# Two transformer blocks in one program: reordered waits, output projections begun with finished pairs, one sum for two norms, modulation summed earlier

## The chip, the core and the metric

The program runs on one core of one Trainium2 chip, as one launch. The metric is the device time in microseconds (us); lower is better. TensorE (PE) multiplies, VectorE (DVE), ScalarE (ACT) and GpSimd (POOL) do elementwise work, SyncE (SP) issues most of the loads. Each engine executes its own instructions in order and waits on semaphores.

## What is computed

A sequence of 256 tokens with 1024 features goes through two blocks of two layers each, all in float32:

```python
# first block
x = x + delta_net(rms_norm(x, a_norm))           # stage A: in-projection, causal conv of 4 taps + silu,
                                                 #   gated delta rule with 8 heads, rms_norm * silu(z), out-projection
k, v = rms_norm(x, kv_norm) @ w_kv               # stage B: one x, two gains
q, z = rms_norm(x, b_norm) @ w_in
x = x + (attention(q, k, v, bias) * silu(z)) @ w_out
x = rms_norm(x, final_norm)
# second block: mod = silu(c) @ ada_w[i] + ada_b[i]; shift, scale, gate = split(mod, 3)
h = rms_norm(x, norm[0]) * (1 + scale) + shift   # stage C
x = x + gate * (retention(rope(q, k), v) * silu(g)) @ w_out
h = rms_norm(x, norm[1]) * (1 + scale) + shift   # stage D: attention with 16 heads, normed q and k
x = x + gate * (attention(...) * silu(g)) @ w_out
```

## The kernel before

**Jobs and chunks.** All arrays lie with features on the 128 partitions. The projections are cut into 104 jobs of 256 output features, numbered through: 0 to 15 in-projection of A, 16 to 19 its out-projection (`JOB_OUT_A`), 20 to 35 in-projections of B (`JOB_B`), 36 to 39 `JOB_OUT_B`, 40 to 63 C, 64 to 67 `JOB_OUT_C`, 68 to 99 D, 100 to 103 `JOB_OUT_D`. A job reads one weight chunk of 1 MB (two in the out-projections of C and D), 112 chunks in all. SP loads chunk c into the buffer `raw` (three slots, so it first waits until chunk c-3 has been split); ACT writes the rounded high part `whi` (`high(c)`, two instructions), DVE the rest `wlo` (`low(c)`, two instructions); both parts have room for two chunks. PE multiplies high by high, high by low and low by high, so a job is 48 matmuls of 256 columns (96 with two chunks), on the two banks ps0 and ps1 in turn. `job(J, ..., ready=, split=)` waits before a tile of its input for `h_ok_sem` or `o_split_sem`. The activations are split in high and low in the same way (`hhi`, `hlo` for the normed input, `ohi`, `olo` for the mixer's output).

**The order is written out by hand.** Each engine has one block of code, and what stands ahead in it runs first. There is no scheduler.

**Stage A.** For job J of 0 to 7 ACT does `high(J + 1)`, the first tap of the convolution of job J (L943), the silu of job J-1 (L948) and for odd J the square of a pair of keys (L953); DVE adds the other three taps (L1283). After each odd job PE sums the squares (`key_sums`). Then comes the delta rule: six levels of a blockwise inversion, each with half of one job before and half behind it (`parts`), over banks that are taken in turn (`slot`, ps6 and ps7). The finished pairs of heads are normed and split by DVE (`split_o`), and `JOB_OUT_A` follows, whose first job waits for each pair.

**Norms.** PE sums the squares of x over the partitions with a matrix of ones (`sums`, `x_sums`), ACT forms the reciprocal root with Ln and Exp (`rsqrt`), DVE scales x tile by tile and takes the rests (`prepare`, L1251 and L1245 or L1247), ACT rounds (`split_h`). In B `prepare` runs twice, with gain `b_norm` and then `kv_norm`, and each run has a `low` of a weight chunk in its middle or behind it. Between B and C two norms follow each other; the kernel forms the squares of x and of x times `final_norm` and two sums, and passes a value from ACT to DVE and back (L1155 to L1162, L1514, L1517). The normed x itself (`final_x`, L1523) is written by DVE during C.

**Attention of B and D, retention of C.** Pair i's softmax, transposes (`turn`, L724) and mixing (`mix`) run during the jobs of pair i+1. After the last pair nothing is left to overlap: PE does `turn` and `mix` and waits for DVE's `finish` (or `finish_c` in C) before the out-projection.

**Modulation.** ada_w is loaded in 48 units of 512 KB into `ring` (two slots). For a unit POOL does one multiply and three adds (`ada_unit`, L373 to L381), PE then one matmul with ones (`ada(u)`), and after six units DVE adds the bias (`take_mod`). SP issues unit u beside a chunk: u of 0 to 17 beside chunks 21 to 38, 18 to 41 beside 40 to 63, the last six in D; unit u waits until POOL has finished unit u-2. POOL starts them after it has spread the two bias tables to DRAM (`scr_d` 4 MB, `scr_b` 2 MB, L391 and L393), read one back and prepared the rope angles (L401 to L426).

## Time and profile before

| what | value |
|---|---|
| median of the runs | 971.07 us |
| the runs | 965.6, 971.07, 971.14 us |
| the profiled execution, its own time | 969.52 us |
| its span on the core | 967.6 us |
| mean granted clock of TensorE | 0.956 of full speed |

The profile comes from one execution. Its span is 1.9 us shorter than that execution's own time; all times inside the trace are counted from the start of the span. Matmul ends are modelled, so only the starts, and the idle time in square brackets before an instruction, are used for TensorE.

### The profile page before, as it was taken

How to read it: one execution, taken by the hardware profiler on the slowest of the kernel's cores; microseconds unless marked ns; L12 is line 12 of the kernel's file. 1: busy time of each engine (PE TensorE's matmuls, PEld its weight loads, DVE VectorE, ACT ScalarE, POOL GpSimd, SP SyncE). 2: the span in 40 equal slices, each digit the busy share in tenths (PEclk: the TensorE clock that was granted, in tenths of full speed). 3: DMA queues.
4: the chain of work that ended last, by engine and by line, in shares of the span. 5: the costliest groups of instructions: out<-in, count | busy, mean ns of one | idle time of the engine just before them, and what ended most of it. 6: DMA issues, size and time to landing. Idle time of an engine off the chain costs nothing.

```text
span 967.6 us, 16171 instructions
## 1 busy us (share of the span) xinstructions
PE 878.0 (91%) x6762; PEld 847.1 (88%) x6762; DVE 586.5 (61%) x803; ACT 478.0 (49%) x736; POOL 299.6 (31%) x238
## 2 busy tenths in 40 slices
PE   4989999999829999789996989699899999999798
PEld 4788899997729999679996989699899999999698
DVE  3675545336696677459977677644567555655643
ACT  4554454444426555345333343423676666766531
POOL 1100000000496878363984767020144300000000
PEclk8997999999979999798997999999999999999999
DMA  6332299542645666154764645285255534425250
GB/s 247 128 130 96 54 142 173 124 116 89 232 153 192 218 244 240 66 196 136 272 226 163 212 171 215 87 282 195 111 189 204 194 136 172 154 109 174 89 189 29
DMA packets 28247, 158.42 MB, mean 164 GB/s; under 512 B 3456, under 2 KB 3984, under 8 KB 13840
## 3 DMA queue, kind: packets, MB, share of 16 engines
q1 hardware_dynamic: 24816, 146.37, 42.3%
q0 software_dynamic: 3360, 11.03, 7.1%
q8 instruction: 53, 0.87, 0.4%
q14 instruction: 18, 0.15, 0.0%
HBM read 150.04 MB, written 7.34 MB: 163 GB/s over the span
## 4 chain that ended last, share of the span: by engine, by line
PE 85%; DVE 9%; ACT 3%; issue 2%; DMA 1%; DVEq 0%; SPq 0%; ACTq 0%
PE ps L448 83%; DVE wlo L1219 2%; DVE arena L1251 2%; PE ps L632 1%; PE ps L724 1%; DVE olo L1264 1%; DVE arena L1538 1%; DVE hlo L1245 1%; ACT whi L874 1%; DMA x<-x_t 1%; DVE ohi L1262 0%; DVE arena L1534 0%; DVE olo L1245 0%; ACT L863 0%; ACT early L953 0%
## 5 line engine op out<-in xcount | busy, mean ns | idle before, releaser
L1219 DVE TENSOR_TENSOR wlo<-raw,whi 128x1024 fp32r<-128x1024 f32 x224 | 310.4, 1423 | 179.2 <-ACT whi L874 179.0
L448 PE MATMUL ps<-hhi,whi 128*128 128x256 f32 x960 | 286.4, 298 | 43.1 <-ACT arena L1097 17.6
L874 ACT ACTIVATE whi<-raw 128x1024 fp32r<-128x1024 f32 x224 | 225.9, 1051 | 106.5 <-PE ps L448 73.6
L448 PE MATMUL ps<-hlo,whi 128*128 128x256 f32 x960 | 278.3, 290 | 0.0
L448 PE MATMUL ps<-hhi,wlo 128*128 128x256 f32 x960 | 277.9, 290 | 0.0
L448 PEld LDWEIGHTS ps<-hhi,whi 128*128 128x128 f32 x960 | 191.4, 199 | 47.0 <-issue 29.0
L448 PEld LDWEIGHTS ps<-hlo,whi 128*128 128x128 f32 x960 | 191.6, 200 | 2.0 <-issue 1.9
L448 PEld LDWEIGHTS ps<-hhi,wlo 128*128 128x128 f32 x960 | 191.0, 199 | 0.0
L448 PE MATMUL ps<-ohi,whi 128*128 128x256 f32 x512 | 149.0, 291 | 16.0 <-DVE olo L1264 11.6
L373 POOL TENSOR_TENSOR ada_ring<-ada_ring,sil 128x1024 f32<-128x1024 f32 x48 | 101.8, 2121 | 170.6 <-DMA ada_ring<-ada 170.6
L448 PE MATMUL ps<-olo,whi 128*128 128x256 f32 x512 | 146.3, 286 | 0.0
L448 PE MATMUL ps<-ohi,wlo 128*128 128x256 f32 x512 | 146.2, 286 | 0.0
L448 PEld LDWEIGHTS ps<-ohi,whi 128*128 128x128 f32 x512 | 99.8, 195 | 18.9 <-DVE olo L1264 11.9
L448 PE MATMUL ps<-arena 128*128 128x128 f32 (+2 forms) x656 | 103.9, 308 | 1.8 <-ACT arena L1079 1.2
L448 PEld LDWEIGHTS ps<-arena 128*128 128x128 f32 x656 | 94.5, 200 | 9.7 <-issue 3.4
L448 PEld LDWEIGHTS ps<-olo,whi 128*128 128x128 f32 x512 | 99.9, 195 | 0.2 <-issue 0.2
L448 PEld LDWEIGHTS ps<-ohi,wlo 128*128 128x128 f32 x512 | 99.7, 195 | 0.0
L448 PE MATMUL ps<-whi,hhi 128*128 128x256 f32 x320 | 94.6, 296 | 0.0
L448 PE MATMUL ps<-wlo,hhi 128*128 128x256 f32 x320 | 90.5, 283 | 0.0
L448 PE MATMUL ps<-whi,hlo 128*128 128x256 f32 x320 | 90.5, 283 | 0.0
L375 POOL TENSOR_TENSOR ada_ring<-ada_ring 128x512 f32<-128x512 f32 x48 | 76.6, 1596 | 3.8
L448 PEld LDWEIGHTS ps<-whi,hlo 128*128 128x128 f32 x320 | 61.4, 192 | 1.9 <-issue 1.9
(190 smaller groups left out, 1045.9 us busy)
## 6 DMA issues: line engine op xcount, KB each, us to landing
raw<-weights SPq DMA_DIRECT2D x112, 1024.0 KB, 5.1
ada_ring<-ada SPq DMA_DIRECT2D x48, 512.0 KB, 5.9
bias_rows_d<-ada_ring POOLq DMA_DIRECT2D x1, 4096.0 KB, 45.9
bias_rows_b<-fb POOLq DMA_DIRECT2D x1, 2048.0 KB, 86.7
arena<-bias_rows_d POOLq DMA_DIRECT2D x2, 1024.0 KB, 10.1
x<-x_t SPq DMA_DIRECT2D x2, 512.0 KB, 4.5
arena<-bias_rows_b POOLq DMA_DIRECT2D x1, 1024.0 KB, 7.1
arena<-bias_rows_d POOLq DMA_DIRECT2D x2, 512.0 KB, 13.3
```

Source lines behind the costliest of these rows:

```text
L373: pool.tensor_tensor(b, b, sil[:, :].unsqueeze(2).to_broadcast([P, KT, P]), ALU.mult).then_inc(ada_step_sem, 1)
L375: pool.tensor_tensor(b[:, 0:4, :], b[:, 0:4, :], b[:, 4:8, :], ALU.add).then_inc(ada_step_sem, 1)
L448: return pe.matmul(o, l, r, start=start, stop=stop, skip_group_check=skip)
L632: m = pe.transpose(b[:, m4 * P:m4 * P + P], tt[:, 4 * g + m4, :], ident)
L724: m = pe.transpose(turned_bank(hh, soft0)[:, a * P:a * P + P], ts[:, hh, c0:c0 + P], ident)
L874: act.activation(whi[:, unit % UNITS, :, :], raw[:, c % RAW, 4 * half:4 * half + 4, :], ACT.Copy).then_inc(hi_ok_sem, 1)
L1219: dve.tensor_tensor(wlo[:, unit % UNITS, :, :], raw[:, c % RAW, 4 * half:4 * half + 4, :], whi[:, unit % UNITS, :, :].bitcast(F32), ALU.su ...
L1245: dve.tensor_tensor(lo[:, t, :], f[:, t, :], hi[:, t, :].bitcast(F32), ALU.subtract).then_inc(h_ok_sem, 1)
L1251: dve.scalar_tensor_tensor(out=f[:, t, :], in0=x[:, t, :], scalar=gain(t), in1=rs, op0=ALU.mult, op1=ALU.mult).then_inc(hf_ok_sem, 1)
L1264: return dve.tensor_tensor(olo[:, r, :], src, ohi[:, r, :].bitcast(F32), ALU.subtract)
L1538: own(dve.scalar_tensor_tensor(out=of[:, t, :], in0=of[:, t, :], scalar=col("ret_gn", 4 * h + k), in1=zs_c[:, 4 * (h % 2) + k, :], op0=ALU ...
```

## The change

1. **Start.** The eight tiles of squares of x are added in pairs by DVE first, so that PE sums four. The first `low` moves behind the first scaled tile.
2. **Key squares.** In jobs 0 to 7 ACT does silu(J-1) and the key square ahead of the first tap of job J.
3. **Modulation.** Units 0 to 29 are loaded from chunk 11 on, three beside a chunk, and summed by POOL before and behind the spreading of the bias tables; PE takes six units at each of the levels 2, 4 and 6 of the delta rule, six after job 17 and six after job 19. `ada_sum` has 12 slots instead of 6. The bias rows lie in memory that `ohi` uses later, so DVE waits for the spread (`scr_out_sem`) before the first `split_o`; reading one table back and the rope angles come behind unit 29. Units 30 to 41 follow in B and its out-projection, none in C; the last six stay in D.
4. **Shared middle input.** x times the root is formed once for B (four instructions of two tiles), and the gains of q and of k/v are applied while ACT rounds and DVE takes the rests; the `low`s in between move ahead or behind.
5. **Out-projections.** The last `turn` and `mix` of B and D are issued inside the first job of the out-projection, before tiles 4 and 6 of B and 8 and 12 of D; that job waits pair by pair. In C the last sum is issued before tile 8.
6. **One sum for two norms.** The product of the two roots is formed from one sum, with the square root of the squared gain plus eps (`gq`) as scale of the square; the plain sum, needed for `final_x` alone, is formed in C from two added tiles; `final_x` moves from h = 0, 1 to h = 1, 2.
7. Several `high` and `low` of the next chunk move ahead of a norm or a finish.

```diff
+        turn_order = ["keys0", "keys1"]
+        for lv in range(1, LEVELS):
+            turn_order += [f"level{lv}_{g}" for g in range(4)]
+            turn_order += {1: ["values0"], 2: ["mod0"], 3: ["values1"], 4: ["values2", "mod1"], 5: ["values3"], 6: ["mod2"]}[lv]
+        turn_order += [f"sum{i}" for i in range(4)]
...
-                    if c == (JOB_B + 1 + u if u < 18 else JOB_C + (u - 18) if u < 42 else 76 + 2 * (u - 42)):
-                        if u < 2:
-                            sp.wait_ge(o_split_sem, 4)
-                            sp.wait_ge(scr_out_sem, 32)
-                        else:
+                    if c == ((11, 11, 12, 12, 12)[u] if u < 5 else 13 + (u - 5) // 3 if u < 26 else u - 6 if u < 42 else 76 + 2 * (u - 42)):
+                        if u >= 2:
                             sp.wait_ge(ada_mul_sem, u - 1)
                         sp.dma_start(ring[:, u % 2, :, :].rearrange("p a b -> p (a b)"), ada_w[u]).then_inc(ada_in[u % 2], 16)
...
-                if u >= 6:
-                    pool.wait_ge(ada_used_sem, u - 5)
-                pool.tensor_tensor(ada_sum[:, u % 6, :], b[:, 0, :], b[:, 1, :], ALU.add).then_inc(ada_mul_sem, 1)
+                if u >= 12:
+                    pool.wait_ge(ada_used_sem, u - 11)
+                pool.tensor_tensor(ada_sum[:, u % 12, :], b[:, 0, :], b[:, 1, :], ALU.add).then_inc(ada_mul_sem, 1)
...
+            pool.wait_ge(sil_ok_sem, 1)
+            pool.wait_ge(conv_ok_sem, 8)
+            for u in range(6):
+                ada_unit(u)
             pool.wait_ge(fd_ok_sem, 2)
             pool.wait_ge(nt_ok_sem, 4)
             pool.dma_start(scr_d.rearrange("p h t -> h p t"), fd[:, :].unsqueeze(1).to_broadcast([16, P, 512])).then_inc(scr_out_sem, 16)
             pool.wait_ge(bias_sb_sem, 1)
             pool.dma_start(scr_b.rearrange("p h t -> h p t"), fb[0:8, :].unsqueeze(1).to_broadcast([8, P, 512])).then_inc(scr_out_sem, 16)
+            for u in range(6, 30):
+                ada_unit(u)
             pool.wait_ge(scr_out_sem, 32)
...
-            for u in range(42):
+            pool.wait_ge(h_ok_sem, 24)
+            for u in range(30, 42):
...
+                            if kx in at:
+                                at[kx]()
+                            if split is not None and kx % heads == 0:
+                                pe.wait_ge(o_split_sem, split + kx // heads + 1)
...
-            def ada(u):
-
-                if u % 6 == 0:
-                    pe.wait_ge(mod_ok_sem, u // 6)
+            def ada(u, bank=ps[7]):
+
+                if u % 6 == 0 and u >= 24:
+                    pe.wait_ge(mod_ok_sem, u // 6 - 3)
                 pe.wait_ge(ada_mul_sem, u + 1)
-                mm(ps[7][:, u % 6:u % 6 + 1], ada_sum[:, u % 6, :], ones[:, 0:1], True, True).then_inc(ada_used_sem, 1)
+                mm(bank[:, u % 6:u % 6 + 1], ada_sum[:, u % 12, :], ones[:, 0:1], True, True).then_inc(ada_used_sem, 1)
...
-            sums(lambda t: xsq_a[:, t, :], 8, S, sq_ok_sem, lambda t: t // 2 + 1)
+            sums(lambda t: xsq_a[:, 4 * (t // 2) + t % 2, :], 4, S, sq_ok_sem, lambda t: t // 2 + 1)
...
+                if lv in (2, 4, 6):
+
+                    b = taken(slot_of_mod(lv // 2 - 1))
+                    for u in range(3 * lv - 6, 3 * lv):
+                        ada(u, b)
...
+                for u in {JOB_OUT_A + 1: range(18, 24), JOB_OUT_A + 3: range(24, 30)}.get(J, ()):
+                    ada(u)
...
+            turn_last, mix_last = attend(JOB_B, 4, 0, 4, (ohi[:, 8:16, :], olo[:, 8:16, :]), (hhi, hlo), False, (8, 16), ada_b)
             for J in range(JOB_OUT_B, JOB_C):
-                job(J, "T", ohi, olo)
-                if J < JOB_OUT_B + 3:
-                    ada(2 * J - 60)
-                    ada(2 * J - 59)
-
-            pe.wait_ge(ss_read_sem, own_ss[0])
-            for t in range(KT):
-                pe.wait_ge(sq_ok_sem, 8 + t + 1 - t % 2)
-                mm(ssb[:, 0:S], ones[:, :], xsq[:, t, :], t == 0, False)
-                pe.wait_ge(sq_ok_sem, 8 + t + 2 - t % 2)
-                m = mm(ssb[:, S:2 * S], ones[:, :], xsq2[:, t, :], False, t == KT - 1)
-            m.then_inc(ss_ok_sem, 1)
-            own_ss[0] += 1
-
+                if J == JOB_OUT_B:
+                    job(J, "T", ohi, olo, split=4, at={4: turn_last, 6: mix_last})
+                else:
+                    job(J, "T", ohi, olo)
+                if J == JOB_OUT_B + 1:
+                    for u in range(39, 42):
+                        ada(u)
+
+            x_sums(2)
...
+                    sums(lambda t: xsq[:, 6 + t, :], 2, S, m1_add_sem, lambda t: 2)
...
+                if J == JOB_OUT_C:
+                    job(J, "T", ohi, olo, split=8, at={8: lambda: sums_c(3)}, heads=4)
...
+                if J == JOB_OUT_D:
+                    job(J, "T", ohi, olo, split=12, at={8: turn_last, 12: mix_last})
...
             for J in range(8):
                 high(J + 1)
-                first_tap(J)
                 if J:
                     silu(J - 1)
                 if J % 2:
                     key_square(J // 2)
+                first_tap(J)
                 if J == 1:
...
+                split_c(J0 + 4 * pairs, 1)
...
+            for dst, gain in ((ohi[:, 8:16, :], "b_norm"), (hhi, "kv_norm")):
+                for t in range(KT):
+                    act.wait_ge(hf_ok_sem, 8 + t // 2 + 1)
+                    act.activation(dst[:, t, :], hf[:, t, :], ACT.Copy, scale=col(gain, t)).then_inc(hh_ok_sem, 1)
...
+            square_x(JOB_OUT_B, gain=lambda t: gq[:, t:t + 1])
...
-            act.activation(rsb[:, 0, :], ssb[:, 0:S], ACT.Ln, scale=1.0 / D, bias=epsc[:, 0:1]).then_inc(fin_ln_sem, 1)
-            act.wait_ge(fin_ln_sem, 1)
-            act.activation(rsb[:, 1, :], rsb[:, 0, :], ACT.Exp, scale=-1.0).then_inc(ss_read_sem, 1)
-            act.activation(rsb[:, 2, :], rsb[:, 0, :], ACT.Exp, scale=-0.5).then_inc(r1_ok_sem, 1)
-            act.wait_ge(fin_mid_sem, 1)
-            act.activation(rsb[:, 3, :], rsb[:, 3, :], ACT.Ln, scale=1.0 / D, bias=epsc[:, 0:1]).then_inc(fin_ln_sem, 1)
-            act.wait_ge(fin_ln_sem, 2)
-            act.activation(rsb[:, 3, :], rsb[:, 3, :], ACT.Exp, scale=-0.5).then_inc(rs_ok_sem, 1)
+            act.activation(rsb[:, 1, :], ssb[:, 0:S], ACT.Ln, scale=1.0 / D, bias=epsc[:, 3:4]).then_inc(ss_read_sem, 1)
+            act.wait_ge(ss_read_sem, ss_n[0])
+            act.activation(rsb[:, 1, :], rsb[:, 1, :], ACT.Exp, scale=-0.5).then_inc(rs_ok_sem, 1)
             split_h(3, hf, hhi, shift=lambda t: mod[:, t:t + 1])
+            for n in range(4):
+                act.activation(xsq[:, 2 * n:2 * n + 2, :], x[:, 2 * n:2 * n + 2, :], ACT.Square).then_inc(m1_sq_sem, 1)
...
+            for t in range(2):
+                dve.wait_ge(xsq_ok_sem, 2 * t + 2)
+                dve.tensor_tensor(xsq_a[:, 4 * t:4 * t + 2, :], xsq_a[:, 4 * t:4 * t + 2, :], xsq_a[:, 4 * t + 2:4 * t + 4, :], ALU.add).then_inc(sq_ok_sem, 1)
             next_rs()
-            low(0)
-            prepare(0, lambda t: col("a_norm", t), None, hf_a, rs_a, hhi, hlo)
+            prepare(0, lambda t: col("a_norm", t), None, hf_a, rs_a, hhi, hlo, between=lambda: low(0), after=0)
...
+            def mod_of_slot(i):
+
+                b, free, n = slot(slot_of_mod(i))
+                dve.wait_ge(ada_used_sem, 6 * i + 6)
+                a0 = COLS["ada_b"] + 6 * i
+                dve.tensor_tensor(mod[:, 6 * i:6 * i + 6], b[:, 0:6], cols[:, a0:a0 + 6], ALU.add).then_inc(free, 1)
...
+                if lv in (2, 4):
+                    mod_of_slot(lv // 2 - 1)
...
+            dve.wait_ge(scr_out_sem, 32)
...
+                    if J in (JOB_OUT_A + 2, JOB_OUT_B + 2):
+                        take_mod(3 if J < JOB_B else 6)
+                    for c in chunks_of(J):
+                        if n or c > chunks_of(J0)[0] or J0 == JOB_OUT_A:
+                            low(c + 1)
...
+                low(chunks_of(J0 + 4 * pairs)[0] + 1)
...
-            prepare(1, lambda t: col("b_norm", t), None, hf, rsb[:, 0, :], ohi[:, 8:16, :], olo[:, 8:16, :])
-            low(JOB_B + 1)
-            prepare(2, lambda t: col("kv_norm", t), None, hf, rsb[:, 0, :], hhi, hlo, between=lambda: low(JOB_B + 2))
+
+            def lo_of(prep, t, gain, hi, lo):
+
+                dve.wait_ge(hh_ok_sem, 8 * prep + t + 1)
+                dve.scalar_tensor_tensor(out=lo[:, t, :], in0=hf[:, t, :], scalar=col(gain, t), in1=hi[:, t, :].bitcast(F32), op0=ALU.mult, op1=ALU.subtract).then_inc(h_ok_sem, 1)
+
+            for n in range(4):
+                dve.tensor_tensor(hf[:, 2 * n:2 * n + 2, :], x[:, 2 * n:2 * n + 2, :], wide(rsb[:, 0, :], 2), ALU.mult).then_inc(hf_ok_sem, 1)
+                if n:
+                    for t in (2 * n - 2, 2 * n - 1):
+                        lo_of(1, t, "b_norm", ohi[:, 8:16, :], olo[:, 8:16, :])
+            for t in (6, 7):
+                lo_of(1, t, "b_norm", ohi[:, 8:16, :], olo[:, 8:16, :])
+            for t in range(KT):
+                lo_of(2, t, "kv_norm", hhi, hlo)
+            low(JOB_B + 2)
...
-            dve.wait_ge(ss_read_sem, rs_n[0] + 1)
-            dve.tensor_tensor(rsb[:, 3, :], ssb[:, S:2 * S], rsb[:, 1, :], ALU.mult).then_inc(fin_mid_sem, 1)
-            dve.wait_ge(r1_ok_sem, 1)
+            low(JOB_C + 1)
...
+                if h in (1, 2):
+                    if h == 1:
+                        dve.wait_ge(r1_ok_sem, 1)
+                    final_x(4 * h - 4)
+                    final_x(4 * h - 3)
```

On the DMA queue of SyncE, from the first weight chunks to chunk 22, before:

```order
L326 DMA raw<-weights 128x2048 x21
L340 DMA ada_ring<-ada 128x1024
L326 DMA raw<-weights 128x2048
L340 DMA ada_ring<-ada 128x1024
L343 DMA arena<-positions 128x256
```

and now:

```order
L340 DMA raw<-weights 128x2048 x11
L351 DMA ada_ring<-ada 128x1024 x2
L340 DMA raw<-weights 128x2048
L351 DMA ada_ring<-ada 128x1024 x3
L340 DMA raw<-weights 128x2048
L351 DMA ada_ring<-ada 128x1024 x3
```

The modulation loads begin with chunk 11 instead of chunk 21, and three of them stand between one weight chunk and the next.

On TensorE, the end of level 2 of the delta rule (four transposes of `tt` and the first matmuls of the job behind), before:

```order
L448 MATMUL ps<-arena 128x64 x4
L632 MATMUL ps<-cst,arena 128x128 x4
L448 MATMUL ps<-hhi,whi 128x256
L448 MATMUL ps<-hlo,whi 128x256
L448 MATMUL ps<-hhi,wlo 128x256
```

and now, with the six matmuls of `ada` between them:

```order
L466 MATMUL ps<-arena 128x64 x4
L652 MATMUL ps<-cst,arena 128x128 x4
L466 MATMUL ps<-ones,ada_sum 128x1 x6
L466 MATMUL ps<-hhi,whi 128x256
L466 MATMUL ps<-hlo,whi 128x256
```

The same six stand at levels 4 and 6; all that PE does behind them waits until POOL has finished the sixth unit.

On ScalarE, one pair of jobs in stage A (L943/L958 first tap, L948/L963 silu, L953/L968 key square, L874/L886 `high`), before:

```order
L874 ACTIVATE whi<-raw 128x1024 x2
L943 ACTIVATE arena<-ps,columns 128x256 x2
L948 ACTIVATE arena<-arena 128x512
L953 ACTIVATE early<-arena 128x512
L874 ACTIVATE whi<-raw 128x1024 x2
```

and now:

```order
L886 ACTIVATE whi<-raw 128x1024 x2
L963 ACTIVATE arena<-arena 128x512
L968 ACTIVATE early<-arena 128x512
L958 ACTIVATE arena<-ps,columns 128x256 x2
L886 ACTIVATE whi<-raw 128x1024 x2
```

The square no longer stands behind the tap that waits for the end of the odd job.

## Rows read from the trace of the kernel before

**Rows 1.** The page, part 1: busy time, share of the span, instructions.

```profile
PE 878.0 (91%) x6762; PEld 847.1 (88%) x6762; DVE 586.5 (61%) x803; ACT 478.0 (49%) x736; POOL 299.6 (31%) x238
```

**Rows 2.** Waits of TensorE: line, releaser, us in total, times, longest.

```profile
PE ps L448 <- ACT early L953: 8.4, 4, 2.1
...
PE ps L724 <- DVE arena L1453: 7.1, 2, 3.6
```

**Rows 3.** Timeline of TensorE after the first key sums, then in full flow: start, us.

```profile
40.13 0.41 PE L448 MATMUL ps<-hhi,wlo 128*128 128x256 f32 x1
40.34 0.41 PE L448 MATMUL ps<-hhi,whi 128*128 128x256 f32 x1
...
50.04 0.28 PE L448 MATMUL ps<-hlo,whi 128*128 128x256 f32 x1
50.16 0.28 PE L448 MATMUL ps<-hhi,wlo 128*128 128x256 f32 x1
```

**Rows 4.** Timeline: last tap of a key convolution, its square, the key sums.

```profile
49.71 0.47 DVE L1283 SCALAR_TENSOR_TENSOR arena<-ps,columns,arena 128x253 f32<-128x253 f32 x1
...
54.02 0.63 ACT L953 ACTIVATE early<-arena 128x512 f32<-128x512 f32 x1
...
54.70 1.05 PE L448 MATMUL ps<-ones,early 128*128 128x1 f32 x8 [2.11 <-ACT early L953]
```

**Rows 5.** The chain that ended last, levels 4 and 6 of the delta rule: start, us.

```profile
170.51 10.13 PE ps L448 x88
...
199.82 26.48 PE ps L448 x206
```

**Rows 6.** Tile raw on the DMA queue of SyncE, 100 to 230 us.

```profile
L326 SPq DMA_DIRECT2D raw<-weights x7: 327/328/328, 118.1 to 207.4; - x7
...
DMA to landing us min/median/max: 5.0/16.9/23.1
```

**Rows 7.** Timeline of SyncE: the load of weight chunk 23.

```profile
251.18 0.33 SPq L326 DMA_DIRECT2D raw<-weights  x1
```

**Rows 8.** The page, part 6: DMA issues, count, KB each, median us to landing.

```profile
ada_ring<-ada SPq DMA_DIRECT2D x48, 512.0 KB, 5.9
bias_rows_d<-ada_ring POOLq DMA_DIRECT2D x1, 4096.0 KB, 45.9
bias_rows_b<-fb POOLq DMA_DIRECT2D x1, 2048.0 KB, 86.7
```

**Rows 9.** Timeline of GpSimd: spread tables, then starts of modulation units.

```profile
116.42 1.11 POOL L391 DMA_DIRECT2D bias_rows_d<-ada_ring  x1 [80.31 <-DVE arena L1349]
...
273.24 2.08 POOL L373 TENSOR_TENSOR ada_ring<-ada_ring,sil 128x1024 f32<-128x1024 f32 x1
...
278.15 1.89 POOL L373 TENSOR_TENSOR ada_ring<-ada_ring,sil 128x1024 f32<-128x1024 f32 x1
...
470.75 2.03 POOL L373 TENSOR_TENSOR ada_ring<-ada_ring,sil 128x1024 f32<-128x1024 f32 x1
...
496.04 2.87 POOL L373 TENSOR_TENSOR ada_ring<-ada_ring,sil 128x1024 f32<-128x1024 f32 x1
```

**Rows 10.** Timeline of VectorE: one step of the second preparation of x.

```profile
284.70 2.11 DVE L1251 SCALAR_TENSOR_TENSOR arena<-x,columns,arena 128x256 f32<-128x256 f32 x1
```

**Rows 11.** Timeline of TensorE: first matmul behind five gaps.

```profile
291.06 0.58 PE L448 MATMUL ps<-hhi,whi 128*128 128x256 f32 x1 [17.65 <-ACT arena L1097]
...
436.81 0.55 PE L448 MATMUL ps<-hhi,whi 128*128 128x256 f32 x1 [6.20 <-DVE hlo L1247]
...
524.74 0.55 PE L448 MATMUL ps<-hhi,whi 128*128 128x256 f32 x1 [7.62 <-DVE wlo L1219]
...
628.20 0.58 PE L448 MATMUL ps<-ohi,whi 128*128 128x256 f32 x1 [6.11 <-DVE olo L1264]
...
917.87 0.39 PE L448 MATMUL ps<-ohi,whi 128*128 128x256 f32 x1 [1.97 <-DVE olo L1264]
```

**Rows 12.** Timeline of TensorE: sum of squares before the middle projections.

```profile
252.01 3.62 PE L448 MATMUL ps<-arena,ones 128*128 128x256 f32 x16
```

More of the change, by code:

```diff
@@ L150, in two_blocks @@
         rt16 = A(9216, 4, S, parts=16)
-        ada_sum = sb("ada_sum", [P, 6, P])
+        ada_sum = sb("ada_sum", [P, 12, P])
         lmask = sb("lmask", [P, LEVELS, 256], U8)
@@ L228, in two_blocks @@
         sq_ok_sem = sem("sq_ok")
+        xsq_ok_sem = sem("xsq_ok")
+        gq_ok_sem = sem("gq_ok")
+        m1_sq_sem = sem("m1_sq")
+        m1_add_sem = sem("m1_add")
         ss_ok_sem = sem("ss_ok")
@@ L455, in bank_empty, with job @@
                     pe.wait_ge(bank_free[J % 2], max(J // 2 - 6, 0))
-            def job(J, form, hi, lo, ready=None, split=None):
+            def job(J, form, hi, lo, ready=None, split=None, at={}, heads=2):
                 bank = v2(pj[J % 2])
@@ L904, in split_h, with square_x @@
                         act.activation(dst[:, t, :], src[:, t, :], ACT.Identity, bias=shift(t)).then_inc(hh_ok_sem, 1)
-            def square_x(J0, second=False):
+            def square_x(J0, gain=None):
                 for n in range(4):
@@ L1195, in _ @@
             attend(JOB_D, 8, 4, 12, True)
-            for J in range(JOB_OUT_D, N_JOBS):
-                for c in chunks_of(J):
-                    high(c + 1)
+            for c in range(chunks_of(JOB_OUT_D)[1], N_CHUNKS):
+                high(c + 1)
         @block.vector
@@ L1238, in wide, with prepare @@
                 return v.unsqueeze(1).to_broadcast([P, n, v.shape[-1]])
-            def prepare(prep, gain, shift, f, rs, hi, lo, between=None):
+            def prepare(prep, gain, shift, f, rs, hi, lo, between=None, after=3):
                 def lo_part(t):
@@ L1253, in prepare @@
                         lo_part(t - 1)
-                    if t == 3 and between is not None:
+                    if t == after and between is not None:
                         between()
@@ L1473, in attend @@
                         lows(J + 1)
-                    if not normed and i == 2:
-                        take_mod(0)
                     lows(J + 2)
@@ L1504, in gains_of_c @@
             def gains_of_c():
-                take_mod(2)
-                dve.wait_ge(mod_ok_sem, 3)
+                for i in range(3):
+                    dve.wait_ge(slot(slot_of_mod(i))[1], slot(slot_of_mod(i))[2] + 1)
                 scaled_gain(0)
```

157 lines of the change are left out of this document (81 added, 76 removed).

## The prediction

> **What bounds the kernel now.** I read the page's busy shares first: TensorE is busy for 878 of 967.6 us, no other engine for two thirds [rows 1]. So the time is what TensorE must do plus what it waits, and the second view is its waits by releaser: four of 2.1 us for key squares and two of up to 3.6 us for the last softmax of B and D [rows 2]; the timeline gives the single long ones, 17.65 us in B (put down to L1097, though the second preparation of x ends just before), 6.2, 7.6, 6.1 and 2.0 us [rows 11]. A gap costs more than its length: behind the first key sums the matmuls of 256 columns start 0.21 us apart, in full flow 0.12 us [rows 3], the two levels of the clock, 1.2 and 2.4 GHz. Such a stretch takes some 12 matmuls, so each gap costs 1 to 2 us behind it. In the delta rule the chain runs through TensorE throughout, a level in 14.7 us [rows 5] (two levels from 170.5 to 199.8). There TensorE has no gap, and everything put in its way there is paid in full.
>
> **Part 1 and 2, start and key squares.** TensorE's 8 sums of float32 squares took 6.0 us at the slow clock; four take 3.0, the two additions of DVE add some 0.7 in front, and the moved low part brings the first matmul forward by about 0.5: gain 2.5 us (estimate). For the key squares the question is whether they can be ready at the end of the odd job. The last tap of the even job's convolution begins at 49.7 and ends at 50.2, and silu and square take about 1.2 us more, so 51.4; the odd job ended at 52.6, 2.1 us before the key sums at 54.7, and the square began only at 54.0 [rows 4]. So all four waits of 2.1 us go, each with its slow stretch (12 matmuls at 0.09 us, and key sums at half speed, together 1.5 us): 4 x 3.6 = 14.5 us. What is late next is the low part for the next job; per pair DVE needs 9.5 us of about 12. Bounds: 8.4 us (the waits alone) and 18. Together with the start the delta rule begins 17 us earlier.
>
> **Part 3, modulation.** Nothing is saved by itself: 48 units before and after, 30 of them now before B. A unit costs GpSimd 4.9 us with a quiet VectorE and 6.3 us beside a busy one (25.3 us for four) [rows 9]; 5.0 to 5.5 in the delta rule. Thirty take 150 to 165 us. The first loads are issued with chunk 11, which I place at 72 us, the first unit is done at 83, the sixth at about 113 (the load of the sixth stands behind chunk 13, which waits for `low(10)`). Only then GpSimd spreads the bias tables, at about 114, nearly the absolute time of before, 116.4 [rows 9], while TensorE is 17 us further on. Level 2 (124 us) finds its six units ready. Level 4 is reached at 170.5 - 17 = 153.5 us [rows 5] and needs unit 11.
>
> The spread is the trouble. While it ran (landed 45.9 and 86.7 us after issue [rows 8], so until 204 us) weight chunks took 5.0 to 23.1 us from issue to landing, median 16.9 [rows 6]; modulation loads in their own, calmer stretch took 5.9 [rows 8]. The ring has two slots, and a load goes out when the unit two before is done, so at a landing time of 16.9 two units pass per 16.9 + 4.9 = 21.8 us. By that alone: unit 7 is done at 124, units 8 and 9 at 143 and 148, 10 and 11 at 165 and 170: level 4 waits 17 us. Level 6 comes 29.3 us later, at 200; unit 17 is done at about 219: 19.7 us. Counting also that a load stands behind its chunk on the one queue (chunk 14 issued at 121 lands at 143, then unit 8 at 149, unit 9 at 155), unit 11 is done at about 181 and unit 17 at 231: 28 and 20 us. After the spread GpSimd keeps pace (unit 23 before the end of job 17). Unit 29, however, is loaded beside chunk 23, and that waits for `low(20)`, which ended at 251.2 us [rows 7], as the last job of the out-projection ended at 252.0 [rows 12]. Load 6, unit 5: TensorE waits 10 to 11 us there in any case, ahead of the sum of squares. Stalls in all: 17 + 19.7 + 10.8 = 47.5 or 28 + 20 + 11 = 59; I take 53, as the truth about the queue lies between, and 4 us for the slow clock behind three stalls. The lower bound is the 11 us alone. That DVE waits for the spread before its first `split_o` costs nothing: the spread ends at 205 to 210, the split comes after the stalls.
>
> The Trainium skill (SBUF — State Buffer, "Who interferes with whom") says that a VectorE instruction with two inputs in SBUF and a GpSimd instruction that reads SBUF lock each other out for their whole length. The trace agrees: a scaling of one tile, 0.47 us elsewhere, took 2.11 us beside a unit [rows 10].
>
> **Part 4, shared middle input.** From the end of the sum of squares at 255.6 [rows 12] to the third job of B at 291.1 [rows 11] passed 35.4 us for two jobs of TensorE. DVE was the bound: 32 tile steps stretched by GpSimd's units (2.11 us for one [rows 10]), and two low chunks between. Now DVE has 4 double steps of 0.69 and 16 of 0.47 us, and units wait for `h_ok` 24, so only the rope angles run beside it, as they did beside the first preparation before. TensorE is then the bound: 2 us to the first matmul, 11.5 for two jobs, 1 to 2 for the slow clock and 1 for the root, 15.8 us. Gain 19.6, less 2 us because the sum of squares now follows a stall at the slow clock, plus 1.7 for the slow start of job 22 in the old order: 19 us. Bounds: 10 (DVE still stretched) and 21.
>
> **Part 5, out-projections.** B: the gaps were 3.6 [rows 2], 0.6 and 2.0 us. Four tiles (2.9 us) cover the first, two more (1.4) the second; the wait for the last pair stays, since two tiles are less than mix and finish. Gain 3.5 and some 1.5 of clock: 5 us. D: eight tiles (5.8 us) and four (2.9) cover all; 5.6 + 1.4 = 7 us [rows 11] (the last gap ended at 917.9). C: gaps of 0.6, 1.3 and 6.1 us, the last before 628.2 [rows 11]; twelve tiles now run ahead of the last pair, and DVE's finish of 5.7 us still leaves some 4 us: gain 5.5 with the units gone from there.
>
> **Part 6, one sum.** Eight fewer sums in the open: 3.5 us. The gap of 6.2 before 436.8 [rows 11] shrinks to the 2.7 of a single root: 3.5. Clock 1, two sums and squares added in C 0.9: gain 7. Bounds 3 and 9. **C itself** has no units left: the 7.6 us before 524.7 [rows 11] came from DVE steps stretched by them as in rows 10: two `final_x` and two low chunks stand there between the finish and the next job, 5.6 us more than undisturbed (estimate). Gain 5.6 and 2.6 of clock; the shorter gap in h = 2 stays, as `final_x` comes there: 8 us.
>
> **Sum**, against the profiled execution (969.5 us of its own, 967.6 span; the median of the runs is 971.1): -17 + 53 + 4 - 19 - 5 - 7 - 8 - 5.5 - 7 = -11.5. From the median: **960 us**.
>
> **Rivals.** (a) *The loads are quick*: the slow landings were those of single 1 MB chunks, and half-size loads slip through in 6 us. Then level 4 and 6 wait for nothing and only the 11 us remain: -17 + 11 + 1 - 19 - 32.5 = -56, 915 us. For it speaks that chunks in that stretch moved in a few us once they began; against it the median of 16.9 us over seven, one of which was issued at 207.4, after the spread [rows 6, 8]. (b) *Half of it*, the stalls at levels 4 and 6 together about 20 us: 937 us. (c) *Each load waits its own turn behind the spread.* If what is queued does not follow at once but pays about 13.5 us again each (21.7 us for a chunk, less the 7 it moves), then between 114 and 205 only some six loads come through, three of them chunks: unit 11 is done at about 211, level 4 waits 57 us, the rest 14: -17 + 71 + 5 - 19 - 32.5 = +8, 979 us. It decides against the change from 62 us of stalls on. Units at 6.3 us throughout would add 10 more: 989. (d) *The gains do not come*: the key waits stay (the squares still late): +14 on the forecast, 974.
>
> The Trainium skill (DMA: Bandwidth & Descriptors, "Queues, rings and completion order") says that each DMA engine takes turns between queues a whole packet at a time, typically 9 to 17 descriptors. That is rival (c) as a mechanism. No row here shows two loads of one queue waiting together, so the trace leaves it open.
>
> **Chances.** Forecast (948 to 970) 0.42; (a) 0.17; (b) 0.17; (c) 0.15 with its worse end; (d) and others 0.09. The range leaves out the fastest third of (a) and the worst end of (c): 912 to 982. A measurement of this kernel tells a change of about 1% from none. Faster by over 1% (below 961.4): (a), (b) and just over half of the forecast, 0.57; within 1%: 0.31; slower: 0.12.
>
> **What the new profile would show.** No wait behind L968's square; a wait of TensorE for GpSimd's `ada_sum` of 15 to 30 us at level 4 (about 154 us), 15 to 20 at level 6 and about 11 after job 19; modulation loads of 12 to 20 us in the spread; in B about 16 us from the root to the third job; no wait over 3 us in h = 1 of C; a gap of 2.7 us before C; no gap over 1 us in D's out-projection. I am wrong if the loads land in 6 us during the spread (then 915), or if unit 11 is done after 190 us.

## The result

The changed kernel takes 977.99 us (median of 5 runs, 974.07 to 979.3), the kernel before 970.35 us (5 runs). The ratio is 1.0079 with a 95% interval of 1.0047 to 1.0112: **slower by 0.8%**, where 960 us, faster by 1%, was forecast. The profiled execution took 977.0 us, its span is 975.2.

The page of the changed kernel, parts 1 and 4 (busy time, the chain that ended last). Against [rows 1] TensorE and VectorE work less, and yet the span is longer. The loads of the modulation now stand in the chain with 8%, GpSimd's four steps with 3, 2, 1 and 1%.

```profile
PE 873.1 (90%) x6742; PEld 843.5 (87%) x6742; DVE 552.6 (57%) x793; ACT 481.0 (49%) x740; POOL 279.1 (29%) x239
...
PE ps L466 71%; DMA ada_ring<-ada 8%; POOL ada_ring L385 3%; DVE wlo L1248 2%; POOL ada_ring L387 2%; POOL ada_ring L389 1%; DVE olo L1293 1%; ACT whi L886 1%; PE ps L751 1%; DVE ohi L1291 1%; DVE arena L1456 1%; DVE arena L1594 1%; ACT L875 1%; DVE hlo L1276 1%; POOL ada_sum L393 1%
```

TensorE's waits in the changed kernel: line, releaser, us in total, times, longest. The key squares of [rows 2] are gone, and of the two waits for the last softmax the one in B has shrunk to 0.7 us and the one in D is gone. One row replaces them, 47.2 us for the modulation sums, and VectorE's last output parts (`olo`) cost 13.4.

```profile
PE ps L466 <- POOL ada_sum L393: 47.2, 6, 20.9
PE ps L466 <- DVE olo L1293: 13.4, 7, 3.9
PE ps L466 <- DVE arena L1298: 8.2, 1, 8.2
PE ps L466 <- DVE hlo L1276: 7.9, 3, 4.6
PE ps L466 <- DVE wlo L1248: 5.3, 3, 2.4
```

**Where the time stands, stage by stage.** The timeline of TensorE has the same landmark instructions in both kernels. The table sets their starts side by side; the difference between two rows of the last column is what the stage between them gained or lost.

| landmark | before | after | after - before |
|---|---|---|---|
| first projection matmul | 18.94 | 16.97 | -2.0 |
| first matmul of the delta rule (L605, now L625) | 115.85 | 102.19 | -13.7 |
| projection in level 4 | 170.27 | 201.75 | +31.5 |
| projection in level 6 | 199.58 | 236.49 | +36.9 |
| first job of A's out-projection | 226.58 | 265.74 | +39.2 |
| sum of squares ahead of B | 252.01 | 312.70 | +60.7 |
| first job of B | 258.18 | 322.32 | +64.1 |
| scores of B's first pair | 304.42 | 346.78 | +42.4 |
| sum of squares ahead of C | 423.54 | 457.61 | +34.1 |
| first job of C [rows 11] | 436.81 | 465.81 | +29.0 |
| behind the shorter middle gap of C | 571.84 | 590.82 | +19.0 |
| first job of D | 682.81 | 697.42 | +14.6 |
| last matmul's end | 964.2 | 971.8 | +7.6 |

Up to the delta rule 13.7 us are gained, from there to B 77.8 are lost, and from B on 56.5 are gained again. Such differences between two single traces are uncertain by 2 to 3 us: two kernels of the experiments below, with the same code up to there, began the delta rule at 98.00 and 100.29 us.

The stalls in level 4, timeline of TensorE of the changed kernel (start, us, in brackets the idle time and its releaser). Three waits, 35.9 us, and then matmuls 0.21 us apart: the granted clock of this stretch (163 to 202 us) is 0.52 of full speed, the lower of the two levels.

```profile
167.61 0.58 PE L466 MATMUL ps<-ones,ada_sum 128*128 128x1 f32 x2 [3.38 <-POOL ada_sum L393]
189.06 0.59 PE L466 MATMUL ps<-ones,ada_sum 128*128 128x1 f32 x2 [20.87 <-POOL ada_sum L393]
201.30 0.58 PE L466 MATMUL ps<-ones,ada_sum 128*128 128x1 f32 x2 [11.65 <-POOL ada_sum L393]
201.75 0.56 PE L466 MATMUL ps<-hhi,whi 128*128 128x256 f32 x1
202.11 0.41 PE L466 MATMUL ps<-hlo,whi 128*128 128x256 f32 x1
202.32 0.41 PE L466 MATMUL ps<-hhi,wlo 128*128 128x256 f32 x1
```

What GpSimd waited for there, from the chain that ended last (start, us, what): a load, the four steps of a unit (4.6 to 6.7 us together), the next load.

```profile
128.70 27.55 DMA ada_ring<-ada
...
156.31 4.04 POOL ada_ring L385
...
163.06 21.32 DMA ada_ring<-ada
...
189.03 16.33 DMA ada_ring<-ada
```

Loads of 512 KB that landed in a median of 5.9 us in [rows 8] took 21.3 to 29.2 us from issue to landing while the spread ran (four, issued from 128 to 168 us; a fifth, issued at 189, took 16.3 and landed as the spread ended at 205), and 3.3 to 5.7 us from then on (issues from 201 us on). Unit 11 was done at 201.

### The profile page after: what moved, and what is told of

The parts are those of the page before. It is cut to its first block, busy times and chain, and to the rows that moved or that the text cites. A ratio compares the mean times of both kernels' runs of the same rounds, so it can differ in the third digit from the quotient of the medians.

```text
span 975.2 us, 16128 instructions
## 1 busy us (share of the span) xinstructions
PE 873.1 (90%) x6742; PEld 843.5 (87%) x6742; DVE 552.6 (57%) x793; ACT 481.0 (49%) x740; POOL 279.1 (29%) x239
## 4 chain that ended last, share of the span: by engine, by line
PE 71%; DVE 8%; DMA 8%; POOL 6%; ACT 3%; issue 2%; SPq 0%; DVEq 0%; ACTq 0%; POOLq 0%
PE ps L466 71%; DMA ada_ring<-ada 8%; POOL ada_ring L385 3%; DVE wlo L1248 2%; POOL ada_ring L387 2%; POOL ada_ring L389 1%; DVE olo L1293 1%; ACT whi L886 1%; PE ps L751 1%; DVE ohi L1291 1%; DVE arena L1456 1%; DVE arena L1594 1%; ACT L875 1%; DVE hlo L1276 1%; POOL ada_sum L393 1%
## 5 line engine op out<-in xcount | busy, mean ns | idle before, releaser
L1248 DVE TENSOR_TENSOR wlo<-raw,whi 128x1024 fp32r<-128x1024 f32 x224 | 294.1, 1352 | 181.1 <-ACT whi L886 181.0
L886 ACT ACTIVATE whi<-raw 128x1024 fp32r<-128x1024 f32 x224 | 225.7, 1052 | 78.6 <-PE ps L466 60.8
L466 PEld LDWEIGHTS ps<-hhi,whi 128*128 128x128 f32 x960 | 189.7, 198 | 22.8 <-issue 21.8
L466 PE MATMUL ps<-ohi,whi 128*128 128x256 f32 x512 | 150.6, 294 | 16.4 <-DVE olo L1293 13.4
L466 PE MATMUL ps<-olo,whi 128*128 128x256 f32 x512 | 148.3, 290 | 0.0
L466 PE MATMUL ps<-ohi,wlo 128*128 128x256 f32 x512 | 148.2, 289 | 0.0
L466 PEld LDWEIGHTS ps<-ohi,whi 128*128 128x128 f32 x512 | 101.8, 199 | 18.9 <-issue 11.2
L466 PEld LDWEIGHTS ps<-olo,whi 128*128 128x128 f32 x512 | 101.9, 199 | 0.0
L466 PEld LDWEIGHTS ps<-ohi,wlo 128*128 128x128 f32 x512 | 101.7, 199 | 0.0
L466 PE MATMUL ps<-arena 128*128 128x128 f32 (+2 forms) x656 | 99.4, 300 | 0.7 <-ACT arena L1219 0.7
L466 PEld LDWEIGHTS ps<-arena 128*128 128x128 f32 x656 | 91.7, 194 | 7.4 <-issue 3.5
L387 POOL TENSOR_TENSOR ada_ring<-ada_ring 128x512 f32<-128x512 f32 x48 | 71.3, 1485 | 3.8
```

Source lines behind the costliest of these rows:

```text
L387: pool.tensor_tensor(b[:, 0:4, :], b[:, 0:4, :], b[:, 4:8, :], ALU.add).then_inc(ada_step_sem, 1)
L466: return pe.matmul(o, l, r, start=start, stop=stop, skip_group_check=skip)
L886: act.activation(whi[:, unit % UNITS, :, :], raw[:, c % RAW, 4 * half:4 * half + 4, :], ACT.Copy).then_inc(hi_ok_sem, 1)
L1248: dve.tensor_tensor(wlo[:, unit % UNITS, :, :], raw[:, c % RAW, 4 * half:4 * half + 4, :], whi[:, unit % UNITS, :, :].bitcast(F32), ALU.su ...
```

## The experiments

**Give the modulation back.** The changed kernel, with the modulation in B and C as before and everything else kept:

```diff
-if c == ((11, 11, 12, 12, 12)[u] if u < 5 else 13 + (u - 5) // 3 if u < 26 else u - 6 if u < 42 else 76 + 2 * (u - 42)):
+if c == (JOB_B + 1 + u if u < 18 else JOB_C + (u - 18) if u < 42 else 76 + 2 * (u - 42)):
...
-                    for u in range(3 * lv - 6, 3 * lv):
-                        ada(u, b)
...
             pool.wait_ge(h_ok_sem, 24)
-            for u in range(30, 42):
+            pool.wait_ge(sil_ok_sem, 1)
+            for u in range(42):
```

> The changed kernel with the modulation as in the kernel before: loads, units, sums and additions all in B and C again, everything else of the change kept. Theory (the moved modulation alone turned the gain into a loss: 45 us of waits and slow clock at levels 4 and 6, 4 in level 1, 10 in the out-projection of A, 14 after it): 978 - 69 = 909, plus about 12 for units that disturb VectorE in C again, 921 us. Rival (the time of the units only changes place, and 42 units beside B and C cost there what they cost in the delta rule): 955 to 975 us.

Measured 931.71 us (928.07 to 934.08), ratio to the kernel before 0.9592 (0.9553 to 0.9631). The moved modulation alone costs 978.0 - 931.7 = 46 us, and the rest of the change gains 38.5. The first theory holds, 11 us off. B's first job begins 79.5 us earlier than in the changed kernel (242.77 us), but the units then cost 15 us between there and C and 16 us behind it, where I had allowed 12. Two waits of VectorE's low part in the middle of C are back, 5.6 and 7.7 us; TensorE's waits:

```profile
PE ps L461 <- DVE wlo L1250: 15.3, 5, 7.7
PE ps L461 <- DVE hlo L1278: 11.9, 5, 7.4
```

From B's first job on, this kernel gains 26 us over the kernel before, where the changed kernel gains 56.5. Stage by stage, by the landmarks of the table: 19.8 us up to the scores of B's first pair, 0.7 from there to C, 1.6 lost in C, 7.0 gained in D. In the changed kernel the same four are 21.8, 13.4, 14.4 and 7.0.

**The key squares alone**, on the kernel before:

```diff
                 high(J + 1)
-                first_tap(J)
                 if J:
                     silu(J - 1)
                 if J % 2:
                     key_square(J // 2)
+                first_tap(J)
```

> The kernel before with only the order of ScalarE changed: silu and key square ahead of the next job's first tap. Theory (the four waits of 2.1 us go, each with its slow stretch): 970.4 - 14 = 956 us, no wait of TensorE for the square. Rival (the low parts or the convolution become late instead, and half of it stays): 963 us or more.

Measured 956.03 us (952.24 to 957.68), ratio 0.984 (0.9802 to 0.9878): 14.1 us under the 970.15 of the kernel before beside it, and no wait for the square is left among TensorE's waits. Four waits of 2.1 us were worth 14, since each had its slow stretch behind it: matmuls 0.21 us apart in the kernel before [rows 3], while here the granted clock from 48 to 60 us, around the second key sums, is 1.00.

**The spread ahead of the units.** The two table spreads go out while the key jobs run:

```diff
+            pool.wait_ge(fd_ok_sem, 2)
+            pool.dma_start(scr_d.rearrange("p h t -> h p t"), fd[:, :].unsqueeze(1).to_broadcast([16, P, 512])).then_inc(scr_out_sem, 16)
+            pool.wait_ge(bias_sb_sem, 1)
+            pool.dma_start(scr_b.rearrange("p h t -> h p t"), fb[0:8, :].unsqueeze(1).to_broadcast([8, P, 512])).then_inc(scr_out_sem, 16)
             pool.wait_ge(sil_ok_sem, 1)
             pool.wait_ge(conv_ok_sem, 8)
             for u in range(6):
                 ada_unit(u)
-            pool.wait_ge(fd_ok_sem, 2)
-            pool.wait_ge(nt_ok_sem, 4)
-            pool.dma_start(scr_d.rearrange("p h t -> h p t"), fd[:, :].unsqueeze(1).to_broadcast([16, P, 512])).then_inc(scr_out_sem, 16)
-            pool.wait_ge(bias_sb_sem, 1)
-            pool.dma_start(scr_b.rearrange("p h t -> h p t"), fb[0:8, :].unsqueeze(1).to_broadcast([8, P, 512])).then_inc(scr_out_sem, 16)
```

> The changed kernel with the spread of both bias tables issued during the key and query jobs, ahead of the first unit, instead of behind the sixth. Theory (the spread delays the loads of units 8 to 11): they land in about 6 us, no wait at level 4 or 6, and GpSimd is far enough ahead that it disturbs A's out-projection less: 978 - 38 - 3 - 4 = 933 us, more if the key jobs now wait for their chunks. Rival (the two ring slots and the one queue with the chunks hold the loads back, the spread matters little): still 20 us or more of waits for the sums, 960 to 978 us.

Measured 947.19 us (945.76 to 949.4), ratio 0.9749 (0.9713 to 0.9786). No wait for a unit is left at levels 4 and 6, and the modulation loads from 85 to 200 us landed in a median of 3.8 us, so the spread is what held them back. The result is 14 us above the 933 expected; they went into the stretch that the spread now fills (34.9 to 125.7 us). The delta rule began 8 us later, and level 2 waited 6.5 us for units 4 and 5. The view of tile `raw`, 15 to 100 us, shows weight chunks that took a median of 15.7 us there (4.9 in the changed kernel):

```profile
DMA to landing us min/median/max: 4.8/15.7/25.1
```

ScalarE waited twice for a chunk, 10.6 us in all, with a key square behind its high part, and TensorE for that square. TensorE's waits:

```profile
PE ps L465 <- POOL ada_sum L393: 17.0, 5, 5.9
PE ps L465 <- DVE olo L1292: 12.7, 5, 3.9
PE ps L465 <- DVE hlo L1275: 7.9, 3, 4.6
PE ps L465 <- ACT early L967: 6.0, 1, 6.0
```

**Does GpSimd itself cost anything?** Units 0 to 5 and 18 to 29 do 2 of their 128 columns in the multiplication and the first two additions (cut below to the multiplication), so the kernel leaves out most of the modulation that these units give:

```diff
-pool.tensor_tensor(b, b, sil[:, :].unsqueeze(2).to_broadcast([P, KT, P]), ALU.mult)
+w = 2 if u < 6 or 18 <= u < 30 else P
+pool.tensor_tensor(b[:, :, 0:w], b[:, :, 0:w], sil[:, :].unsqueeze(2).to_broadcast([P, KT, w]), ALU.mult)
```

> The changed kernel in which units 0 to 5 and 18 to 29 multiply and add 2 of 128 columns only (their last addition is whole), so this part of the modulation is left out; loads, waits and semaphores stay. Theory (GpSimd's large instructions hold up VectorE's): the wait before level 1 falls from 3.3 to 1.1 us, the two-column copy from 1.76 to 0.2 us, the three gaps in A's out-projection from 6.8 to about 1.5 us; with the slow clock behind them 978 - 10 = 968 us, some more where the last units come sooner. Rival (these gaps come from what was late before them, not from GpSimd): they stay, 975 to 978 us.

Measured 960.05 us (957.03 to 961.38), ratio 0.9882 (0.9847 to 0.9917): 18 us less than the changed kernel, more than the 10 expected. TensorE's waits for the sums are the same as there (46.8 against 47.2 us), so it isn't theirs, and what is shorter among TensorE's direct waits is VectorE's:

```profile
PE ps L467 <- POOL ada_sum L394: 46.8, 6, 21.5
...
PE ps L467 <- DVE olo L1294: 7.9, 5, 3.9
...
PE ps L626 <- DVE arena L1388: 1.1, 1, 1.1
```

By the landmarks 1.4 us of the gain lie ahead of the delta rule and 16.0 between its start and B's first job: 4.1 up to the first sum of level 4, 9.0 in the first two jobs of A's out-projection, 2.7 behind them; 1.8 are lost again behind B's first job. About half of the 16.0 are shorter waits; the rest lies in part in the stretches behind them, as from 270.9 to 273.8 us in the changed kernel, where the granted clock is 0.50.

The same four steps of A's output on VectorE, first in the changed kernel, then here. Scaling, cast and low part took 1.83 + 1.38 + 1.09 us beside the units and 0.69 + 0.43 + 0.69 without; only the first step, which reads PSUM, is the same. A pair took 5.25 us instead of 3.0, and TensorE, done with a pair in 2.9 us even at the lower clock (270.90 to 273.82), waited each time.

```profile
270.94 0.75 DVE L1452 SCALAR_TENSOR_TENSOR arena<-ps,columns,arena 128x512 f32<-128x512 f32 x1
271.73 1.83 DVE L1456 TENSOR_TENSOR arena<-arena 128x512 f32<-128x512 f32 x1
273.59 1.38 DVE L1291 CAST ohi<-arena 128x512 fp32r<-128x512 f32 x1
275.00 1.09 DVE L1293 TENSOR_TENSOR olo<-arena,ohi 128x512 fp32r<-128x512 f32 x1
```

```profile
263.98 0.75 DVE L1453 SCALAR_TENSOR_TENSOR arena<-ps,columns,arena 128x512 f32<-128x512 f32 x1
264.77 0.69 DVE L1457 TENSOR_TENSOR arena<-arena 128x512 f32<-128x512 f32 x1
265.49 0.43 DVE L1292 CAST ohi<-arena 128x512 fp32r<-128x512 f32 x1
265.95 0.69 DVE L1294 TENSOR_TENSOR olo<-arena,ohi 128x512 fp32r<-128x512 f32 x1
```

Ahead of level 1 it is a copy of two columns that stands on the path. In the changed kernel it began with a GpSimd multiplication (96.81, 1.90 us) and ended with it; here it took a tenth. First GpSimd and VectorE in the changed kernel, then VectorE in this one:

```profile
96.81 1.90 POOL L385 TENSOR_TENSOR ada_ring<-ada_ring,sil 128x1024 f32<-128x1024 f32 x1
...
96.97 1.76 DVE L1385 COPY ecol<-early 128x2 f32<-128x2 f32 x1 [2.62 <-ACT early L1015]
```

```profile
97.79 0.17 DVE L1386 COPY ecol<-early 128x2 f32<-128x2 f32 x1 [5.21 <-ACT early L1016]
```

**Later deadlines.** Units 0 to 17 keep their place in GpSimd's order, but TensorE sums 6 to 17 only in A's out-projection. Units 18 to 29 move too: 18 to 22 behind the last split of A, the others and all of their sums into B. So the run changes the deadline of the first and the place of the second:

```diff
+LOAD_AT = [11, 11, 12, 12, 12, 13, 13, 13, 14, 14, 16, 16, 18, 18, 19, 19, 19, 19, 20, 20, 21, 22, 23, 24]
+LOAD_AT += [u + 2 for u in range(24, 34)] + [36, 36, 37, 37, 38, 38, 39, 39] + [76 + 2 * k for k in range(6)]
+SUM_AT = {16: range(6, 12), 18: range(12, 18), 25: range(18, 24), 29: (24, 25), 30: (26, 27), 31: (28, 29),
+          34: (30, 31), 35: (32, 33), 36: (34, 35), 38: range(36, 40), 39: (40, 41)}
...
-                if lv in (2, 4, 6):
+                if lv == 2:
```

> The changed kernel with the units where they were until unit 17, but TensorE sums only units 0 to 5 in the delta rule (level 2); 6 to 11 are summed after job 16, 12 to 17 after job 18, the rest in B. Loads follow fewer per chunk; GpSimd starts unit 18 after the last split of A, units 23 to 41 after B's preparation. Theory (what cost the time is the early deadline, not the work of the units): no wait at levels 4 and 6 (-37 -2 us and 3 of slow clock), none after job 19 (-12), the first gaps of A's out-projection back to about 1 us (-8), some 5 us more in B for seven further units: 921 us, below the kernel with the old modulation (931.7). Rival (the loads hold up the chunks behind them on the one queue, and TensorE waits for weights instead at level 6 and in A's out-projection): 935 us or more.

Measured 936.88 us (934.98 to 939.27), ratio 0.9659 (0.9623 to 0.9694). That is 41 us under the changed kernel, but 16 above the 921 expected and in the rival's range. The waits at levels 4 and 6 and after job 19 are gone, and no matmul waited for weights at level 6 or in A's out-projection, so the rival's number came without its mechanism. What was missing is VectorE again: A's out-projection had gaps of 1.5, 3.7 and 2.3 us (units 14 to 16 ran beside VectorE's steps), the preparation of B waited 8.5 us, and level 1 was no faster than in the changed kernel. Against the kernel with the old modulation 25 us are lost between the start of the delta rule and B, and 22 gained behind it. Levels 4 and 5 took 14.87 us each, as in the kernel before; two units, 8 and 9, ran beside them (158.7 to 169.5 us), and there they were free.

**Is B's preparation faster because GpSimd is kept away?** The wait for B's inputs is taken from the kernel with the old modulation:

```diff
-            pool.wait_ge(h_ok_sem, 24)
```

> The kernel e1_old_mod (931.7 us) without the wait that holds the first unit until B's inputs are ready, so that units run beside B's preparation as they did in the kernel before. Theory (a good part of the gain there is that GpSimd is kept away, since scaling and low parts have two SBUF inputs): the third job of B begins 5 to 9 us later, 937 to 940 us. Rival (the fewer and wider steps alone are the gain, TensorE is the bound there anyway): the same, 930 to 933 us.

Measured 931.32 us (928.12 to 932.98), the same as the 931.71 there. The rival's number came, but the experiment says less than planned: the rope angles on GpSimd last until 254.4 us and the preparation ends at 259.1, so only the first unit meets it, and only its last three low parts (4.43 us for the three). The third job of B begins 14.0 us after the first instead of 12.9. What the wait protects here is about 1 us, which the runs don't tell from none; what units beside the whole preparation would cost stays open.

**A better distribution.** From the kernel with the old modulation: six units in the delta rule (the first begins at 100.8 us, inside level 1), twenty beside B, none in C while `final_x` and a finish are due:

```diff
+LOAD_AT = [12, 12, 14, 14, 16, 16] + list(range(21, 41)) + [43, 43, 44, 45, 46, 47, 48, 49, 49, 50, 55, 56, 60, 61, 62, 63] + [76 + 2 * k for k in range(6)]
...
+            pool.wait_ge(sil_ok_sem, 1)
+            pool.wait_ge(tp_ok_sem, 4)
+            for u in range(6):
+                ada_unit(u)
             pool.wait_ge(scr_out_sem, 32)
```

> The kernel e1_old_mod (931.7 us) with its units distributed otherwise: six of them run in the delta rule, from the end of level 1 on, and are summed only after job 18; twenty beside B; of those beside C none while VectorE has final_x and a finish to do. Theory (a unit costs only where VectorE is late, or where TensorE waits for its sum, and neither holds between level 1 and the last split of A): nothing in the delta rule, the gaps of 5.6 and 7.7 us in C shrink to about 2.3 each, with their slow clock 10 us less: 922 us. Rival (the gaps of C are those of final_x and finish alone, and the six loads in the spread hold up chunks): 930 to 936 us.

Measured 925.85 us (924.87 to 929.21), ratio 0.9542 (0.9518 to 0.9567). That is 4 us above the 922 expected. C's two gaps fell from 5.6 and 7.7 to 1.76 and 2.38 us as expected, the delta rule took as long as without units (A's out-projection begins at 208.74 us in both traces), but a new wait of 5.86 us stood behind job 25, where all of units 6 to 11 are summed:

```profile
PE ps L467 <- DVE hlo L1290: 14.2, 7, 7.4
...
PE ps L467 <- POOL ada_sum L396: 6.3, 2, 5.9
```

**The second chunk's split in the middle of the preparation** (on top of that, `high` and `low` of the second chunk of B, C and D moved behind the fourth tile):

> e7_spread_units with the split of the second chunk of B, C and D put in the middle of the preparation of the input again, instead of ahead of it. Theory (ScalarE's high part, 2.0 us, and VectorE's low part, 2.4 us, stand between the root and the first scaling, so TensorE starts late): 2 us less in each of B and C, nothing in D: 4 us under e7. Rival (the second job then waits for its chunk as long as the first one gained): the same as e7.

Measured 927.75 us (925.99 to 930.82), ratio 0.9555 (0.9529 to 0.9581), against 0.9542: the rival holds. The gap ahead of C fell from 7.4 to 4.2 us, and one of 3.2 came behind it, before the matmul at 418.25 us, 9.7 us after C's first; D got a new one of 3.3 us.

**The sums of units 6 to 11 apart**, in the list of units that TensorE sums behind a job of B:

```diff
-for u in range(6, 12) if J == 25 else range(J - 18, J - 17) if J >= 30 else ():
+for u in (6, 7) if J == 25 else range(J - 18, J - 17) if J >= 26 else ():
```

> e7_spread_units (925.9 us) with the sums of units 6 to 11 taken after jobs 25 to 29, two and then one at a time, instead of all six after job 25, where TensorE waited 5.9 us for the last of them. Theory (the wait is the deadline alone, the units are there two jobs later): the wait and about 1.5 us of slow clock behind it go, 918 to 920 us. Rival (units beside the first jobs of B are so slow that the wait comes again one or two jobs on): 924 to 926 us.

Measured 922.99 us (919.55 to 924.49), ratio 0.9489 (0.9456 to 0.9523). The wait for the sums is gone; half of it came back as 2.1 and 0.9 us for VectorE in the same place. Between the two numbers expected, this is the fastest version: **4.8 to 5.4% under the kernel before**, 55 us under the changed kernel.

## Why the prediction was wrong

**Start and key squares (forecast -17): right in the mechanism, 3 us too much.** The last matmul ahead of the delta rule ended 15.9 us earlier, and the key order alone gave 14.1 us. Of the 15.9, 2.2 were lost again: the first wait of the delta rule was 3.33 us instead of 1.12, behind the copy L1385 that a unit held up.

**Modulation (forecast +53 and +4 for the clock, measured +77.8): the step that failed.** The waits themselves came as forecast: 47.2 us in all against 47.5 to 59. They lay otherwise than I had them, 35.9 at level 4, 2.1 at level 6 and 9.3 after job 19, since four loads in the spread took 21 to 29 us and not the 16.9 that I took as the middle of the weight chunks. Unit 11 was done at 201 us; in this the trace is nearer to rival (c), in which each load waits its own turn, but its 71 us of waits did not come, because two loads waited together and the spread was over at 205. The Trainium skill (DMA: Bandwidth & Descriptors, "Queues, rings and completion order") has the engines take turns between queues by whole packets. The trace fits it in that a unit of 512 KB and a chunk of 1 MB, both of 128 rows, waited about as long when they stood first in line (21.3 and 21.8 us); no run here tells this cause from others. The prediction's own bound, unit 11 after 190 us, marked it as wrong.

What I did not count is what the units do to VectorE. This is the term that the sum put at nothing: I priced the units by TensorE's waits for `ada_sum` alone, with part 4 already saying that a VectorE step took 2.11 us beside a unit instead of 0.47 [rows 10]. The light units put 18 us on it (16.0 of them inside this stretch, by the traces): the start of the delta rule, level 1, and three waits in A's out-projection with their slow stretches. The Trainium skill (SBUF — State Buffer, "Who interferes with whom") says it of more than the two-input steps that I quoted: copies and casts can use the shared ports too. The trace agrees, with the cast of 0.43 us that took 1.38 and the copy of 0.17 that took 1.76. The remaining 14.6 us of the 77.8 are in part five groups of sums at 1.3 us each, which leave B and C, and slow stretches behind the stalls (1.9 us behind level 4, 3.0 in the sum of squares); some 3 us are not placed. (A gap of 1.4 us in level 3, for which the profile shows no releaser, is absent with the light units and so part of their 16.) The sums side by side: forecast -17 + 57 - 51.5 = -11.5, measured -13.7 + 77.8 - 56.5 = +7.6.

**From B on (forecast -51.5, measured -56.5): the sum right, its division only in part.** Shared middle input -21.8 against -19 (now 24.5 us from the first job to the scores, before 46.2; counted from the sum of squares, as the forecast was, -18.3); B's end and the preparation of C -13.4 against -12; the middle of C -10.0 against -8; its end -4.4 against -5.5; D -7.0 against -7. The gap ahead of C is 4.6 us, not 2.7, as the low part L1248 now stands ahead of the first scaling. That units had stretched C is shown: with them back, its gaps were 5.6 and 7.7 us, without them at those places 1.8 and 2.4.

The agreement is partly luck. With the modulation back in B and C the rest of the change gained only 26 us from B on, so 30 of the 56.5 come with the units' absence: 6.5 are their sums, 8.6 the two gaps in C, 3.9 the gap ahead of C with two small ones behind it; the rest, slow stretches among it, is not placed. The prediction said of the modulation that nothing is saved by itself, and credited the absence with the 8 us of C and a part of the 5.5 behind it. For parts 5 and 6 it claimed 12 us between B's scores and C, where only 0.7 came while the units were there (the gap ahead of C was then 7.4 us). How much each of these parts gives by itself was not measured. The 19.8 us of the shared input did come with units back in B, and the 7.0 in D, where all kernels have the same six.

**Rivals.** (a) and (b) fall with the 35.9 us at level 4. (d) falls with the key squares alone. (c) was nearer with unit 11 (211 us against 170 to 181, measured 201) and had the waits wrong; that its 979 us lies beside the measured 978 is luck. The range, up to 982, held the result, but the sign was wrong, with 0.57 on faster.

## What to carry to other kernels

Work that moves to an idle stretch of an engine had three prices here, and the wait for its result was only the first (47 us). The second is what it does to a neighbour whose instructions grow longer beside it, on whichever of them are late (16 to 18 us). Look through the destination for such steps, small ones too; here two columns were enough. The third is that its loads come late, if a large transfer of another queue runs there. And count what the old place gains when the work leaves it: here 30 us, of which the forecast had less than half.

Set the deadline apart from the place: two units beside levels 4 and 5, and six in the whole delta rule in the better distribution, cost nothing there once their sums were read later; units beside the split of A's output did cost.

## What was not expected of the hardware

Four loads of 512 KB took 21.3 to 29.2 us beside the spread of 4 and 2 MB, no less than the 1 MB chunks did (21.8 and 27.2 us in the same stretch): the size of the load hardly mattered. Transfers in line behind one another landed 6.0 to 6.2 us apart, chunk or unit (at 150.1, 156.2 and 162.3 us, and at 184.4, 190.6 and 196.6).

A VectorE copy of two columns took 1.76 us instead of 0.17 and ended with the GpSimd multiplication beside it. In the kernel with later deadlines the same copy began 0.75 us into such a multiplication (97.83 against 97.08 us), took 1.17 and ended with it again. So most of its time was the rest of the other engine's instruction, and not its own work.
